# A two-block transformer on one core: stick-breaking attention in the stacked form, and the edges of gating, merge and experts

## The reference, cut to what matters

```
def stick_breaking_attention(q, k, v):          # per block of 128 queries
    z = einsum('bqhd,bshd->bhqs', qb, k) * scale
    mask = kpos[None, :] < tpos[:, None]
    log_keep = where(mask, log_sigmoid(-z), 0)
    after = cumsum(log_keep, axis=3, reverse=True) - log_keep
    a = where(mask, exp(log_sigmoid(z) + after), 0)
    return einsum('bhqs,bshd->bqhd', a, v)
...
y_b = gelu(gu) * (W_s layernorm(gelu(gv)) + b)                          # spatial gating
m = sigmoid(ga) * (y_a @ w_pa) + sigmoid(gb) * (y_b @ w_pb); m @ w_out  # merge
sum over experts e of g_e * gelu(u_e . h) * v_e                         # peer
```

## Time and profile before

| | us |
|---|---|
| median of three runs | 3156.18 |
| profiled execution, its own time | 3159.31 |
| its span in the trace | 3157.9 |
| TensorE busy | 3016.5 (96%) |
| VectorE busy | 2249.8 (71%) |
| ScalarE busy | 1325.6 (42%) |
| GpSimd busy | 803.4 (25%) |
| mean granted TensorE clock | 0.976 |

### The profile page before, as it was taken

The page is one execution under the profiler, slowest core; times in us unless marked ns, Lnnn a source line. Parts: engine busy times, 40 slices in busy tenths (PEclk is TensorE's granted clock), DMA queues, the critical chain, the costliest instruction groups (busy, mean ns, idle before and its releaser), DMA issues. The chain is left out here.

```text
span 3157.9 us, 43286 instructions
## 1 busy us (share of the span) xinstructions
PE 3016.5 (96%) x16184; PEld 2615.3 (83%) x16184; DVE 2249.8 (71%) x4366; ACT 1325.6 (42%) x2320; POOL 803.4 (25%) x696
## 2 busy tenths in 40 slices
PE   7999899999999999979989989999999999999998
PEld 5666688887777788857768868999999999999997
DVE  4767576775885867753443368978788888988886
ACT  3656432233664322333432234348844333344333
POOL 1000100001001200041000124678734444424431
PEclk9999899999999999979999989999999999999999
DMA  4001144333222443211122223655699999999993
GB/s 146 24 28 58 54 167 144 132 110 104 92 82 100 153 147 134 102 59 56 44 70 94 94 80 105 193 180 232 232 356 331 320 340 332 341 323 321 330 329 114
DMA packets 189711, 525.34 MB, mean 166 GB/s; under 512 B 15792, under 2 KB 80176, under 8 KB 187200
## 3 DMA queue, kind: packets, MB, share of 16 engines
q1 hardware_dynamic: 130432, 308.84, 28.6%
q0 software_dynamic: 45104, 164.68, 14.8%
q10 hardware_dynamic: 13968, 49.06, 4.0%
HBM read 484.22 MB, written 38.31 MB: 165 GB/s over the span
## 5 line engine op out<-in xcount | busy, mean ns | idle before, releaser
L239 PE MATMUL bank<-h_hi,w_hi 128*128 128x512 f32 (+1 forms) x2528 | 965.0, 382 | 47.7 <-ACT w_hi L207 14.0
L239 PE MATMUL bank<-h_lo,w_hi 128*128 128x512 f32 (+1 forms) x2528 | 945.5, 374 | 0.0
L213 DVE TENSOR_TENSOR w_lo<-w_raw,w_hi 128x1024 fp32r<-128x1024 f32 (+1 forms) x452 | 580.6, 1285 | 293.7 <-ACT w_hi L207 291.1
L207 ACT ACTIVATE w_hi<-w_raw 128x1024 fp32r<-128x1024 f32 (+1 forms) x508 | 545.3, 1074 | 507.7 <-PE bank L239 487.4
L239 PEld LDWEIGHTS bank<-h_hi,w_hi 128*128 128x128 f32 x2528 | 482.9, 191 | 136.8 <-issue 36.9
L239 PE MATMUL bank<-h_hi,w_lo 128*128 128x512 f32 (+1 forms) x2528 | 593.2, 372 | 0.1
L239 PEld LDWEIGHTS bank<-h_lo,w_hi 128*128 128x128 f32 x2528 | 484.0, 191 | 57.9 <-issue 2.2
L239 PEld LDWEIGHTS bank<-h_hi,w_lo 128*128 128x128 f32 x2528 | 459.4, 189 | 63.4 <-issue 6.1
L239 PE MATMUL bank<-e_hi,w_hi 128*128 128x384 f32 x1024 | 345.5, 337 | 11.1 <-DVE e_lo L2503 11.1
L239 PE MATMUL bank<-e_lo,w_hi 128*128 128x384 f32 x1024 | 344.7, 337 | 0.0
L2411 POOL DMA_INDIRECT own_row<-in_u_rows,own_e x128 | 166.7, 1303 | 268.3 <-DVE sums L2540 214.8
(11 more groups left out here) (418 smaller groups left out, 4417.4 us busy)
## 6 DMA issues: line engine op xcount, KB each, us to landing
w_raw<-in_w SPq DMA_DIRECT2D x476, 512.0 KB, 3.8
ada_w<-in_ada_w POOLq DMA_DIRECT2D x48, 512.0 KB, 3.5
expert_weights<-G ACTq DMA_DIRECT2D x12, 2048.0 KB, 7.2
Gin<-expert_weights SPq DMA_DIRECT2D x32, 768.0 KB, 9.9
w_raw<-in_w SPq DMA_DIRECT2D x32, 704.0 KB, 4.0
hidden_ahead<-u_stage ACTq DMA_DIRECT2D x56, 192.0 KB, 3.9
ahead<-hidden_ahead SPq DMA_DIRECT2D x28, 384.0 KB, 7.0
fx_crow<-fox_cum POOLq DMA_DIRECT2D x8, 512.0 KB, 4.1
```

What stands on the lines that cost most here:

```text
L207: sc.activation(w_hi[s][:, 0:n], w_raw[raw_slot[u]][:, 0:n], ACT.Copy).then_inc(*w_hi_made.next(u))
L213: ve.tensor_tensor(w_lo[s][:, 0:n], w_raw[raw_slot[u]][:, 0:n], w_hi[s][:, 0:n], ALU.subtract).then_inc(*w_lo_made.next(u))
L239: m = te.matmul(out, wt, moving, start=(not low and k == 0 and moving is hi), stop=(low and k == len(blocks) - 1))
```

## The change

- **Stick breaking** uses the stacked form: the units come as key, query, values; scores are two matmuls over 128 rows per head; PE waits for "k lo" and "q lo" at a pair's first step. The turn of v moves into the next pair's step 0. PT holds a whole pair, and the sums are four matmuls per head at its end. In the last pair 12 yields (36 matmuls) of the first two out-projection units run between the steps, and the splits of the second are at its steps 1 and 2. Several buffers are shared with others (`hf`, `acc`, `nv`).
- **Neighbour to gating:** the splits of V[2] are in neighbour's step 16, where VectorE also copies the banks of V[0] and V[1] to `hf`; the gelus read the copies. `after(te, before)` is gone in gating.
- **Gating to merge:** the sigmoid table is loaded and both first gates are taken in gating. Merge's ScalarE waits for gating's end only ahead of its first m_hi.
- **Experts:** four `af` buffers; in the first block e_hi and e_lo of the hidden tiles are delayed (none in units 0 to 2, two each in 3 to 5, one each in 6 and 7); tile 7's own rows run after e_lo in all blocks; SP fetches six weights ahead of the stage and the seventh between the halves of Gin.

```diff
@@ -1385,6 +1242,8 @@
         split_lo(U[0] + 1)
         yield
         ve.wait_ge(*w_used.at(U[0]))
+        if p:
+            ve.wait_ge(*pe.at(name, "v turned", p - 1))
...
+    def stick(before, st, o_hi, o_lo, ready, order):
+        U = [take(3) for _ in range(4)]
+        V = take(KT)
+        begun = ahead_units(V, o_hi, o_lo, ready, order)
+        B = stacked_buffers(st, "sb", hf[0], hf[1], hf[1])
+        q, k_hi, k_lo, qf, kf, v, vT = B
+        neg = acc
...
+        PT = [sb(st, f"sb_pt{hh}", [P, 3 * TT + 1, P]) for hh in range(2)]
...
+        def sums_of(p):
+            for hh in range(2):
+                te.wait_ge(*act.at("sb moved", hh, 4 * p + TT - 1))
+            te.wait_ge(*act.at("sb", "ready", p))
+            if p >= 2:
+                te.wait_ge(*dve.at("sb out", p - 2))
+            for j in range(TT):
+                for hh in range(2):
+                    rows = head_rows(hh)
+                    t = te.matmul(o_banks[p % 2][rows, j * P:T], v[p % 2][:, TT - 1 - j, rows], PT[hh][:, 4 * j:3 * j + TT, :], start=(j == 0), stop=(j == TT - 1))
+                    if j == TT - 1:
+                        t.then_inc(*pe.next("sb sums", hh, p))
...
+                if i == 0 and p < 4:
+                    more = pair_units(p + 1) if p < 3 else itertools.chain(itertools.islice(begun[0], 7), itertools.islice(begun[1], 5))
+                    a, b, c = (2, 2, 2) if p < 3 else (1, 1, 0)
+                for hh in range(2):
+                    if m < steps:
+                        if i == 0:
+                            te.wait_ge(*dve.at("sb", "k lo", p))
+                            te.wait_ge(*dve.at("sb", "q lo", p))
+                        if m:
+                            te.wait_ge(*dve.at("sb z", hh, m - 1))
+                        stacked_scores(s_bank[hh][:, 0:kw], q[p % 2], k_hi[p % 2], k_lo[p % 2], hh, slice(i * P, (i + 1) * P),
+                                       slice(T - kw, T)).then_inc(*pe.next("sb scores", hh, m))
+                run(more, a)
+                if m >= 2:
+                    for hh in range(2):
+                        te.wait_ge(*act.at("sb probs", hh, m - 2))
+                        for j in range(i2 + 1):
+                            t = te.transpose(t_bank[hh][:, (i2 - j) * P:(i2 - j + 1) * P], Pm[hh][m % 2][:, j * P:(j + 1) * P], ident[:, :])
+                        t.then_inc(*pe.next("sb turned", hh, m - 2))
+                if i == 0 and m < steps:
+                    turn_values(U[p], B, "sb", p)
+                run(more, b)
+                if m >= 2 and i2 == TT - 1:
+                    sums_of(p2)
+                run(more, c if i < TT - 1 or p >= 3 else 1 << 30)
...
+                if p == 3 and i == 1:
+                    split_hi(V[1])
...
+                if i == 0 and m < steps:
+                    take_values(U[p], B, "sb", p)
+                run(more, 1)
...
+                if p == 3 and i == 2:
+                    split_lo(V[1])
...
                     split_hi(V[1])
+                if p == 4:
+                    split_hi(V[2])
...
                     split_lo(V[1])
+                if p == 4:
+                    split_lo(V[2])
+                    for j in range(2):
+                        ve.wait_ge(*w_used.at(V[j]))
+                        ve.tensor_copy(hf[j][:, :], lin[V[j] % 2][:, :]).then_inc(*dve.next("gv raw", j))
+                        bank_of.taken(V[j], dve)
...
+    def gate_scalar(name, n, u, dst):
+        sc.wait_ge(*w_used.at(u))
+        if n:
+            sc.wait_ge(*dve.at("merged", n - 1))
+        sc.activation(dst[:, :], lin[u % 2][:, :], ACT.Sigmoid).then_inc(*act.next(name, n))
+        bank_of.taken(u, act)
...
         def tensor():
-            after(te, before)
...
             for k, u in enumerate(V):
-                if k:
+                if k > 1:
                     split_hi(u + 1)
-                sc.wait_ge(*w_used.at(u))
-                sc.activation(gv[:, k, :], lin[u % 2][:, :], ACT.Gelu_apprx_tanh).then_inc(*act.next("gv", k))
-                bank_of.taken(u, act)
+                if k < 2:
+                    sc.wait_ge(*dve.at("gv raw", k))
+                    sc.activation(gv[:, k, :], hf[k][:, :], ACT.Gelu_apprx_tanh).then_inc(*act.next("gv", k))
+                else:
+                    sc.wait_ge(*w_used.at(u))
+                    sc.activation(gv[:, k, :], lin[u % 2][:, :], ACT.Gelu_apprx_tanh).then_inc(*act.next("gv", k))
+                    bank_of.taken(u, act)
...
                 sc.activation(vn[:, n, :], t_bank[n % 2][:, :], ACT.Copy).then_inc(*act.next("vn", n))
+            sc.preload_act_table_set("sigmoid_and_others")
+            gate_scalar("ga", 0, merge_a, hf[0])
...
                 sc.activation(y_hi[:, k, :], mix[k % 2][:, :], ACT.Copy).then_inc(*act.next("gm hi", k))
+            gate_scalar("gb", 0, merge_b, hf[1])
...
             after(ve, before)
-            for u in V[1:]:
+            for u in V[2:]:
...
         U = [take(3) for _ in range(KT)]
-        ga = sb(st, "ga", [P, T])
-        gb = sb(st, "gb", [P, T])
+        ga, gb = hf
...
         def scalar():
-            after(sc, before)
-            sc.preload_act_table_set("sigmoid_and_others")
             for n, (ua, ub, uc) in enumerate(U):
-                for name, u, dst in (("ga", ua, ga), ("gb", ub, gb)):
-                    if n:
-                        split_hi(u + 1)
-                    sc.wait_ge(*w_used.at(u))
-                    if n:
-                        sc.wait_ge(*dve.at("merged", n - 1))
-                    sc.activation(dst[:, :], lin[u % 2][:, :], ACT.Sigmoid).then_inc(*act.next(name, n))
-                    bank_of.taken(u, act)
+                if n:
+                    split_hi(ua + 1)
+                    gate_scalar("ga", n, ua, ga)
+                    split_hi(ub + 1)
+                    gate_scalar("gb", n, ub, gb)
                 split_hi(uc + 1)
+                if n == 0:
+                    after(sc, before)
...
         Gin = sb(st, "Gin", [P, G_BATCH, H8, G_TOK])
-        af = [hf[j][:, 0:TD] for j in range(2)]
+        af = [hf[j][:, 0:TD] for j in range(2)] + [ny[:, 0:TD], sb(st, "hidden3", [P, TD])[:, :]]
...
         quarters = [sb(st, f"ahead{s}", [P, 2, TD]) for s in range(2)]
-        own_a = sb(st, "own_a", [P, SLOTS])
-        own_w = sb(st, "own_w", [P, SLOTS])
+        own_a, own_w = acc_c[:, 0:SLOTS], acc_c[:, SLOTS:2 * SLOTS]
...
             order.append((g, j))
-            if len(order) > 2:
-                sc.wait_ge(*dve.at("e", *order[-3]))
-            sc.activation(af[j % 2], src, ACT.Gelu_apprx_tanh).then_inc(*act.next("gelu", g, j))
+            if len(order) > 4:
+                sc.wait_ge(*dve.at("e", *order[-5]))
+            sc.activation(af[j % 4], src, ACT.Gelu_apprx_tanh).then_inc(*act.next("gelu", g, j))
...
             sc.wait_ge(*dve.at("weighted", g, j))
-            sc.activation(hi[:, j, :], af[j % 2], ACT.Copy).then_inc(*act.next("e hi", g, j))
+            sc.activation(hi[:, j, :], af[j % 4], ACT.Copy).then_inc(*act.next("e hi", g, j))
         def hidden_lo(g, j, hi, lo, own, n):
-            f = af[j % 2]
+            f = af[j % 4]
...
                              Gin[:, :, j, :], ALU.mult).then_inc(*dve.next("weighted", g, j))
-            run(own, n)
+            if j < KT - 1:
+                run(own, n)
...
             ve.tensor_tensor(lo[:, j, :], f, hi[:, j, :], ALU.subtract).then_inc(*dve.next("e", g, j))
+            if j == KT - 1:
+                run(own, n)
+        def weighted_by(i, j):
+            return max(0, min(j + 1, 2 * j - 4)) if i == 0 else j + 1
...
                     bank_of.taken(u, act)
-                    hidden_hi(g, j, e_parts[0][0])
-                    own_rows_done()
-                    done += 1
+                    for j2 in range(weighted_by(i, j - 1), weighted_by(i, j)):
+                        hidden_hi(g, j2, e_parts[0][0])
+                        own_rows_done()
+                        done += 1
...
                         run(own, start)
-                    hidden_lo(g, j, *e_parts[0], own, used_by(done) - used_by(done - 1))
-                    done += 1
+                    for j2 in range(weighted_by(i, j - 1), weighted_by(i, j)):
+                        hidden_lo(g, j2, *e_parts[0], own, used_by(done) - used_by(done - 1))
+                        done += 1
...
-            fetch_weights(whole[0][1][:5])
+            fetch_weights(whole[0][1][:6])
...
             fetch_g(AHEAD, 0, None)
+            fetch_weights(whole[0][1][6:7])
             fetch_g(AHEAD, 1, None)
-            fetch_weights(whole[0][1][5:])
+            fetch_weights(whole[0][1][7:])
...
             nsa("attn0", s2, o_hi, o_lo)
+        even_blocks = (lambda k: dve.at("sb out", k) if k < 4 else dve.at("nsa out", k - 4)), (4, 5, 6, 7, 0, 1, 2, 3)
         with ExitStack() as s2:
-            stick("nsa", s2, o_hi, o_lo)
```

(6 more changed lines are left out.)

## The result

The changed kernel takes 3127.16 us in the median of four runs (3120.91 to 3129.35), beside 3155.31 us (3153.09 to 3157.96) for the kernel before: a ratio of 0.9898, interval 0.9886 to 0.9910. The profiled execution took 3128.80 us with a span of 3127.3, so against the profiled 3159.31 it is 30.5 us shorter; by the medians it is 28.2 us. Forecast were 3123 (3115 to 3134 for the likeliest case) and 32.8 us off the profiled execution.

A forecast was written before the change was run, and what follows sets the result against it. TensorE, busy 96%, was taken as the bound; 8.0 + 6.7 + 3.8 + 4.0 + 10.3 = 32.8 us off 3159.3 gives 3126.5, or 3123 as median; range 3115 to 3134 (0.61), bounds 3108 to 3142.

The forecast's parts named there:

- Pair 0: First stick-breaking pair: TensorE sets its pace, 24.3 us against 26.65, and 2.1 saved before its first score; together −4.5.
- The walk: Middle stick-breaking pair summed step by step from starts of z: 29.86 us against 28.85, step 4 to 5 unchanged at 6.98.
- Rival (2): Stick-breaking pairs: a gap of about 4 us at each pair's end drops the clock, 9 more, about 3132 us; chance 0.15.
- a granted clock under 0.9: Stick-breaking pairs: a granted clock falling under this value would show the forecast wrong.
- rival (1): Stick-breaking pairs: TensorE's pace holds, 24.3 us instead of 29.9 in two pairs, −11.2, about 3112 us; chance 0.11.
- The last pair and the out projection: End of stick breaking: pair 2.3 us longer; 156 matmuls left of 192, 37.3 us against 46.4, −9.1.
- Sum of the stage: Stick breaking with out projection: −4.5 + 2.0 + 2.3 − 9.1 = −9.3 us, taken as −8 for clock losses, bounds −3 and −20.
- Gating and merge: Entries of both stages: idle and slow matmuls behind it saved, 6.7 us at gating and 3.8 at merge.
- Experts' entry: Experts' first block: 7.2 us of wait and slow matmuls saved, 3.3 given back; taken as 4.0, bounds 0 and 7.
- e_lo: Experts' blocks: e_lo ahead of own rows removes nearly all TensorE's waits for it, 10.3 us, bounds 5 and 10.9.
- rival (3): Experts: savings come back as other waits, w_lo being late; 12 of 14.3 lost, about 3135 us; chance 0.09.
- rival (4): Stick-breaking pairs: the clock doesn't come back within a pair, +18.7 us each, three times +56: 3179; chance 0.04.

The follow-up runs named there:

- key_lo in one half: Changed kernel, but key_lo made only in the half that meets q_hi, the other half zero; median 3117.70 us, ratio 0.9875.
- the first fill: Changed kernel, but twelve matmuls of the next key unit ahead of first scores in pairs 1 and 2, six of out projection in pair 3; ratio 0.9902.
- o_hi first: Changed kernel, but ScalarE copies o_hi ahead of key_hi at a pair's second step; ratio 0.9908.
- products first: Changed kernel, but in units 3 to 5 of the experts' first block VectorE makes both products, then own rows, then both e_lo; median 3122.79 us.
- the edges alone: Kernel before with only the new entries of gating and merge; ratio 0.9968.

## Why the forecast held, point by point

- **Scores level.** Four stacked matmuls of 512 columns start 0.23 us apart in after (304.81, 305.04, 305.28, 305.51), 1.1 us for both heads as with the four pieces before. The form given up did what the rule of the Trainium skill ("TensorEngine Tiling (Array Packing)", Performance Considerations) asks for, and the trace agrees with it. Cut off at 306.10 us, the timeline of before shows two of the four pieces in 0.70 us, and both have started by 305.70; I read them as one per head, on its 64 rows:

```profile
305.65 0.70 PE L1035 MATMUL bank<-sb_k,sb_q 64*128 64x512 f32 x2
```

The next two start at 306.18. So a plain fp32 piece takes 0.53 us and two run at once, and a stacked matmul takes 0.23 and runs alone: what the stacking gives up, its shorter matmuls give back. The forecast had the two forms level from their rows and didn't say why.
- **Pair 0.** 23.75 us (24.3 forecast), and its first score 2.2 us earlier (2.1). The gain against 26.65 is partly luck: in the profiled execution of before the clock fell in this pair (0.94), and in the three other executions with the old form it takes 25.1.
- **A middle pair.** The walk's steps 5 to 6, 6 to 7 and 7 to the next 4 were 8.47, 6.78 and 7.63; measured were 8.34, 6.76 and 7.79. The step that failed is the one it called unchanged, 4 to 5: 6.98 became 8.02. TensorE's gap of 3.3 us in front of it dropped the clock, its transposes ran at the lower pace, and ScalarE's weight split and VectorE's w_lo waited behind them. Rival (2) named this mechanism. Its size was over-stated: about 1.0 us a pair and not 2 to 3, because a pair has 5 us to spare on TensorE and only the transposes' delay reaches VectorE. Of the idle 5.5 us that the forecast gave TensorE, 3.3 were left: its 24.3 us of work took 27.65. The forecast had named a granted clock under 0.9 in the pairs as a sign that it is wrong, and it was 0.89: the mechanism of rival (2) was there, and only its low price left the total inside the range. The rule that the forecast took from the Trainium skill ("TensorE: Matmul & The Clock Gate", Why this matters for your kernels) agrees with all twelve long gaps here; that the fall costs little where TensorE isn't the bound is what these runs add.
- **The pace of a fox pair, rival (1).** It fell: with VectorE relieved of 1.4 us the pair shrank by 1.7 plus the clock's 1.0, so VectorE's order was the bound.
- **The last pair and the out projection.** +2.9 (2.3) and, up to the norm, 48.39 against 57.02, −8.6 (9.1). Of the rest, 0.90 us is a wait for the third unit's w_hi, a split that has to wait until the first unit is used. I had written no cost there.
- **Sum of the stage.** −6.9 in this trace, −7.5 in two others; −8 was forecast, −9.3 before the allowance for the clock.
- **Gating and merge.** 6.8 and 4.4 against 6.7 and 3.8. From mix to merge's first matmul it is 2.45 us less (9.56 to 7.11), as the idle of 2.29 said; of the other 2.0, 1.6 is the slow pace (from merge's first matmul to the next unit's 7.23 us before, 5.62 after), put at 1.5, and 0.35 is a shorter wait ahead of norm2 (2.47 to 2.12) that I hadn't in the sum. The kernel with stick breaking alone has this too, so it isn't the edges'.
- **Experts' entry.** The term was 4.0 and measured 2.1; it was 3.0 in seven other executions with this part, and 1.7 in the one with key_lo in one half. The stalls were right in place and nearly in size (0.95 and 1.91 for 0.85 and 2.45). What the sum left out is that the second of them starts a slow stretch of its own, as it did in this execution and in those seven: ten matmuls at 0.32 in place of 0.17 apart cost 1.5.
- **e_lo.** 10.7 against 10.3, with some luck: 1.6 of it is one block of the kernel before in which TensorE ran slowly behind the wait (70.2 us for 68.6). What took the wait's place, rival (3), came to 1.1 us for x in three blocks and 0.6 for the own rows' sums.
- **The slower case, rival (4),** fell: the middle pairs' granted clock was 0.89, and full speed was back within 6.6 us of the first scores (252.05 to 258.6).
- **The total.** The five terms sum to 32.8 and measured 30.9; +0.6 us came in untouched stages. It is a balance: in the neighbour attention the same gap of 2.03 us was followed by the lower clock in this execution alone, and the stretch behind it took 106.96 us where the thirteen others have 104.3 to 104.4; up to that gap after is 2.0 us shorter. By the medians the change took off 28.2 us, where the forecast had some 33.

## What to carry to other kernels

Walk the slower engines' queue step by step from starts in the trace; it gave three of four steps within 0.2 us, though the busy shares alone (VectorE 71%) said nothing. Then look at each gap that the walk leaves on TensorE and ask what runs right behind it, since its first matmuls may come at half pace. When a fill or a reorder is tried, keep the phase of what follows, and look for what stands behind the moved instruction on its own engine; three of four such edits here (the first fill, o_hi first, products first) only moved the stall.

## What the hardware showed beyond that

- In the stacked form the clock fell behind every gap of 3.3 us and more in front of a pair (twelve in the table, and those of the last pairs), and also behind gaps of 1.83, 2.10, 2.36 and 2.92 us, but not behind others of 2.12 and 2.33. A gap of 2.03 us in the neighbour attention was followed by a fall once in fourteen executions. In the old form the two short stops in front of a pair (0.79 and 0.69 us) were followed by one in some executions: in the kernel with the edges alone the first steps of pairs 1 and 2 took 8.32 and 8.33 us, in the kernel before 6.98 and 6.99. The stalls of 1.7 to 2.0 us at the experts' V units, five in each of the four executions with the old order, were followed by a slow stretch in six of twenty cases (70.2 to 71.6 us where 68.6 is usual). Where e_lo comes first these stalls are gone, and between the V units such a stretch was seen only once, behind the 2.73 us of the kernel with the products first. So for the shorter gaps the length alone doesn't decide, and taking such a stall away is worth on average more than its length.
- The time up to nsa's end, untouched by any kernel, lay anywhere from 205.26 to 211.92 us in 14 profiled executions. That is most of the 8 us by which executions of one kernel differ, and it goes with the clock: from 30 to 205 us the granted clock was 0.93 in the two longest (211.80 and 211.92), 0.95 to 0.97 in ten and 0.98 in the two shortest (205.26 and 205.58), while the waits of over 1.2 us behind the first matmul were the same in all. Why the clock differed there stays open.
